# Indirect DMAs in place of the gather and scatter products of seven expert units

## The chip, the cores and the metric

The kernel runs on one core of a Trainium2 chip. The metric is the device time of one execution in microseconds (us).

## The reference, cut to what matters

Two transformer layers on 256 tokens of width 1024 with 16 meta tokens ahead of them. The second layer ends in a top-2-of-8 mixture of experts, and then a final RMSNorm:

```python
logits = (x @ w_router).astype(jnp.float32)
top_v, top_i = lax.top_k(logits, TOP_K)
gates = jax.nn.softmax(top_v, axis=-1)
combine = jnp.sum(jax.nn.one_hot(top_i, N_EXPERTS) * gates[..., None], axis=1)
for e in range(N_EXPERTS):
    out = out + combine[:, e:e + 1] * _swiglu(x, w_gate[e], w_up[e], w_down[e])
```

All numbers are float32; an expert has 1024 x 3584 gate and up weights and 3584 x 1024 down weights.

## The kernel before

All weights stream from HBM once, in chunks of 128 x 4096 numbers (2 MB), through three buffers `raw`. ScalarE rounds a chunk to fp32r (`wh`, L627 for the experts), VectorE subtracts and rounds the rest (`wl`, L993), and TensorE (PE) makes three products with the rounded parts of the activations: high by high, high by low, low by high. `wh` and `wl` have two buffers each. SP issues the next load into a `raw` buffer as soon as VectorE has finished with it (L374 for the experts).

Layer 0 and the attention of layer 1 go first. GpSimd does nothing there but issue a few loads of constants. Then the router's logits are made, each token's two best experts are found, and each token gets its place among the tokens of each expert (`pos`, 1 to 128 within a unit, 0 for none). This ends with the semaphore `routed`.

The experts are worked through in units. A unit is one expert with up to 128 of its tokens; an expert with more tokens gets a further unit, so there are 8 to 11 of them, and their number is read from memory as `units`. The loop over units runs on PE, ScalarE, VectorE and SP at once, one body each, tied by semaphores that count per unit. A unit has 21 chunks, in the order g0, u0, then g, u and d of the one before for six rounds, then d6 in two halves (22 pieces). In one unit, on PE:

- `up(i, "g")` and `up(i, "u")` (L1610, L1611, L1616): gate and up products of one chunk, 24 matmuls of 512 columns. ScalarE makes SiLU of the one, VectorE multiplies with the other (L1131).
- `turn(i)` (L1653): four transposes of that activation, rounded into `eah` (ScalarE, L662) and `eal` (VectorE).
- `down(i)` (L1630, L1631, L1638): 24 matmuls into PSUM banks 2 and 3.
- `gather(u + 1, half)` (L1586): the next unit's tokens, as columns. The tokens `tok` lie in SBUF as rows; a 0/1 matrix `pick` that VectorE builds from `pos` (L1046) is the other operand. Each half is 16 matmuls; half 0 stands after the fourth turn of activations, half 1 after the last. ScalarE and VectorE round the result into `gh` and `gl`.
- the scatter (L1685): the unit's output `y`, copied from banks 2 and 3 by ScalarE (`output_out`, L657), is multiplied by `payT`, which holds each token's gate at its slot. Four fp32 products go to PSUM and VectorE adds them into `acc` (`add_unit`, L1113), while the next unit runs. `payT` comes from `pay` (VectorE, L1146) by two transposes (L1669) and a copy (L686).

PE works in order. At a unit's end it runs gather half 1, both halves of d6, waits for ScalarE's copy of `y`, runs the four scatter products and begins the next unit. ScalarE's order at that place is: rounding of piece 0 of the next unit, `output_out`, rounding of piece 1. VectorE's is: subtraction of piece 0, one of the four additions, subtraction of piece 1, and the other three additions later.

Of the kernel before, what the change touches and what calls it, by code (L numbers as in the profile page):

```python
# [26 lines left out]
F32 = mybir.dt.float32  # L27
# [17 lines left out]
E = 8  # L45
# [39 lines left out]
MAX_UNITS = E + 3  # L85


SUMS = (4, 7, 5, 6)
# [28 lines left out]
def constants():  # L117

    r = np.arange(P)
    ident = np.eye(P, dtype=np.float32)  # L120
    from_here = (r[:, None] >= r[None, :]).astype(np.float32)
    ones = np.ones((P, P), np.float32)
    before = (r[:, None] < r[None, :]).astype(np.float32)
    strict = np.where(r[:, None] < r[None, :], np.float32(0), np.float32(MASKED)).astype(np.float32)
    causal_bias = np.zeros((P, L), np.float32)
    causal_bias[:, L - P:] = np.where(r[None, :] <= r[:, None], 0.0, MASKED)
    swap = np.zeros((P, P), np.float32)
    swap[r, r ^ 32] = 1.0
# [6 lines left out]
    return {  # L135
        "c_base": np.concatenate([ident, ones], 1),
        "c_stick": np.concatenate([-from_here, -ones, ident, strict[:, 0:KT2[2]], strict], 1).astype(np.float32),
        "c_diff": np.concatenate([causal_bias, swap, cos, sin], 1).astype(np.float32),
        "c_route": np.concatenate([before, slots, desc, E - desc], 1).astype(np.float32),
    }  # L140


def build(nc, x, meta, gains, sb_qkv, sb_o, d_qkv, d_o, subln, lq1, lk1, lq2, lk2,
          ffn_gate, ffn_up, ffn_down, router, moe_gate, moe_up, moe_down, final_norm,
          c_base, c_stick, c_diff, c_route, out):
    ctx = ExitStack()
    with ctx:
# [27 lines left out]
        wr = sb("wr", [P, KD, E])  # L175
        xn3 = xn[:].rearrange("p (k t) -> p k t", t=L)
        nd = DIFF_HEADS * SEQ

# [38 lines left out]
        def experts(own):  # L217
            b = {}
            for name, shape in (("tok", [P, QT, D]), ("acc", [P, QT, D]), ("pick", [P, QT, P]), ("pay", [P, QT, P]),
                                ("payT", [P, SEQ]), ("sil", [P, BANK]), ("act", [P, BANK]), ("y", [P, D]),  # L220
                                ("r", [P, 10, QT, E]),
                                ("one", [P, 8, QT]), ("pos", [P, QT, 12]), ("gate", [P, QT, 12]),
                                ("over", [P, 20, E]), ("unit_f", [P, 16])):
# [3 lines left out]
            b["unit_i"] = sb("unit_i", [1, 16], I32, where=own)  # L227
            return b

# [53 lines left out]
        y_ev, sc_done, acc_done = sem("y_ev"), sem("sc_done"), sem("acc_done")  # L283
        fin_sq, fin_root, fin_ready = sem("fin_sq"), sem("fin_root"), sem("fin_ready")

        def cols(w, i):
# [106 lines left out]
        @block.gpsimd  # L393
        def _(pool):
            pool.dma_start(soft_row[:, 0:3 * P + DIAG], c_stick).then_inc(stick_in, 16)
            pool.dma_start(rcon[:], c_route).then_inc(route_in, 16)
            pool.dma_start(wr[:], router[0].rearrange("(k p) e -> p k e", p=P)).then_inc(route_in, 16)

            pool.wait_ge(w_used, C_D_QKV)
            pool.dma_start(b1["con"][:], c_diff).then_inc(diff_in, 16)  # L400

            pool.wait_ge(logit_done, 1)
            pool.wait_ge(back_done, 8)
            pool.dma_start(xn[:, 0:D], final_norm[None, :].to_broadcast([P, D])).then_inc(gain_in, 16)


        @block.scalar
        def _(act):
# [250 lines left out]
            with act.Fori(0, units) as u:  # L659
                def turned_high(i):  # L660
# [3 lines left out]

                with act.If(u > 0):
                    unit_split(u, 0)
                    output_out(u)
                    unit_split(u, 1)
                for j, (kind, i) in enumerate(unit_chunks):
# [10 lines left out]
                    if kind == "d" and i + 1 < FC:  # L680
                        turned_high(i + 1)
                        if i + 1 == FC - 1:
                            unit_split(u, PIECES - 1)
                        if i + 1 == 3:
                            act.wait_ge(payT_done, u + 1)
                            act.copy(bm["payT"][:], ps[:, 7, 0:SEQ]).then_inc(payT_ev, 1)  # L686
                        if i + 1 == FC - 1:

                            gathered_high(u + 2)

            output_out(units)
# [12 lines left out]
        def _(dve):  # L704
# [396 lines left out]
            step(ins)  # L1101
            dve.wait_ge(routed, 1)
# [3 lines left out]
            dve.nop().then_inc(acc_done, 4)  # L1106
# [8 lines left out]
            with dve.Fori(0, units) as u:  # L1115
# [4 lines left out]
                with dve.If(u > 0):  # L1120
                    unit_split(u, 0)
                    add_unit(u, 0, 1)
                    unit_split(u, 1)
                for j, (kind, i) in enumerate(unit_chunks):
# [9 lines left out]
                    if j + 2 < CPU:  # L1134
                        unit_split(u, j + 2)
                    if (kind, i) == ("u", 0):
                        with dve.If(u > 0):
                            add_unit(u, 1, 4)
                    if kind == "d" and i + 1 < FC:
                        turned_low(i + 1)  # L1140
                        if i + 1 == FC - 1:
                            unit_split(u, PIECES - 1)
                        if i == 1:

# [3 lines left out]
                            ins.then_inc(pay_ready, 1)  # L1148
                        if i == 2:
                            dve.wait_ge(gathered, u * 2 + 2)  # L1150
                            pick(u + 1)
                        if i + 1 == FC - 1:
                            gathered_low(u + 2)
            add_unit(units, 0, 4)

# [10 lines left out]
        def _(pe):  # L1166
# [426 lines left out]

            pe.nop().then_inc(sc_done, 4)
            pe.wait_ge(routed, 1)
            units = pe.value_load(bm["unit_i"][0:1, 15:16], min_val=E, max_val=MAX_UNITS)
            with pe.Fori(0, units) as u:
                gh, gl = bm["gh"], bm["gl"]
# [20 lines left out]
                def down(i, k0=0, n=4):  # L1619
# [23 lines left out]
                def turn(i):  # L1643

                    pe.wait_ge(eprod_ready, u * FC + i + 1)
                    if i:
                        pe.wait_ge(eal_ready, u * FC + i)
                    else:

# [6 lines left out]
                for i in range(FC):  # L1656
# [5 lines left out]
                    if i >= 1:  # L1662
                        down(i - 1)
                        turn(i)
                    if i == 3:
                        pe.wait_ge(pay_ready, u + 1)
# [4 lines left out]
                    if i == 4:  # L1671

                        gather(u + 1, 0)

                gather(u + 1, 1)
                down(FC - 1, 0, 2)
                down(FC - 1, 2, 2)
                pe.wait_ge(payT_ev, u + 1)

                pe.wait_ge(gl_ready, u * 2 + 4)  # L1680
                for n in range(4):
                    half, t = n // 2, n % 2
                    if t == 0:
                        pe.wait_ge(y_ev, u * 2 + half + 1)
                    pe.matmul(ps[:, SUMS[n], :], bm["payT"][:, t * P:(t + 1) * P],  # L1685
                              bm["y"][:, half * BANK:(half + 1) * BANK], start=True, stop=True).then_inc(sc_done, 1)


# [19 lines left out]
```

## Time and profile before

| | |
|---|---|
| time, median of 3 runs | 1607.09 us (1605.15 to 1608.3) |
| the profiled execution | 1607.7 us, its span 1605.5 us |
| granted TensorE clock, mean of the span | 0.981 |
| PE, VectorE, ScalarE, GpSimd busy | 1542.0, 1170.3, 938.6, 3.4 us |
| weights' queue | 422.79 MB |
| unit starts, the first matmul of the first and of the last | 562.5 and 1466.1 us |

The span runs from the first to the last instruction of the execution that was profiled; the time of that execution is 2.2 us longer. "Busy" is the union of an engine's instructions. PE stands for matmuls, PEld for its weight loads, DVE for VectorE, ACT for ScalarE, POOL for GpSimd, SPq for the queue of SyncE from which the weights are loaded. An arrow in brackets names what ended an engine's idle time.

### The profile page before, as it was taken

The page shows a single profiled execution, that of the slowest core. Times are in us where ns is not written, and L with a number is a line of the kernel's source. Part 1 is how long each engine was busy: PE and PEld are TensorE (multiplying, and loading weights), DVE is VectorE, ACT ScalarE, POOL GpSimd, SP SyncE. Part 2 cuts the span into 40 slices and gives each one's busy share as a digit, 9 for nine tenths or more (in the row PEclk, how much of TensorE's full clock was granted, in tenths as well). Part 3 has the DMA queues.
Part 4 walks back from the last instruction along what each step waited for, and adds up shares of the span by engine and source line. Part 5 has one row for each costly group of instructions (what it writes and reads, how often), then busy time and mean ns, then how long its engine had stood idle before and what let it go on. Part 6 is the DMA issues. An engine that isn't in the chain of part 4 may idle for free.

```text
span 1605.5 us, 21014 instructions
## 1 busy us (share of the span) xinstructions
PE 1542.0 (96%) x8451; PEld 1311.4 (82%) x8451; DVE 1170.3 (73%) x927; ACT 938.6 (58%) x674; POOL 3.4 (0%) x9
## 2 busy tenths in 40 slices
PE   4999999998987999999999999999999999999997
PEld 4999999998975978878878878878887887887885
DVE  4545756536765578788878878878878878787886
ACT  4454543524236566576666666666666656666664
POOL 0000000000000000000000000000000000000000
PEclk9999999999987899999999999999999999999999
DMA  7444353552530289999989999989999998998993
GB/s 200 119 145 158 128 187 108 210 197 103 209 106 1 81 310 341 347 329 358 343 324 352 344 335 355 366 292 357 337 332 350 370 344 298 361 348 324 359 337 122
DMA packets 198057, 424.93 MB, mean 265 GB/s; under 512 B 3737, under 2 KB 30522, under 8 KB 198010
## 3 DMA queue, kind: packets, MB, share of 16 engines
q1 hardware_dynamic: 197568, 422.79, 73.1%
q0 software_dynamic: 384, 1.45, 0.3%
q8 instruction: 35, 0.57, 0.2%
q14 instruction: 12, 0.10, 0.0%
q10 hardware_dynamic: 58, 0.02, 0.0%
HBM read 423.19 MB, written 1.05 MB: 264 GB/s over the span
## 4 chain that ended last, share of the span: by engine, by line
PE 85%; DVE 7%; ACT 4%; DMA 3%; issue 1%; SPq 0%; DVEq 0%; ACTq 0%
PE ps L1610 12%; PE ps L1611 12%; PE ps L1616 12%; PE ps L1638 6%; PE ps L1190 6%; PE ps L1631 6%; PE ps L1630 6%; PE ps L1181 5%; PE ps L1180 5%; DMA raw<-in_moe_w_down 3%; DVE wl L993 2%; PE ps L1685 2%; PE ps L1586 2%; PE ps L1249 1%; PE ps L1653 1%; DVE wl L720 1%
## 5 line engine op out<-in xcount | busy, mean ns | idle before, releaser
L993 DVE TENSOR_TENSOR wl<-raw,wh 128x4096 fp32r<-128x4096 f32 (+1 forms) x176 | 744.5, 4230 | 167.4 <-ACT wh L627 156.7
L627 ACT CAST wh<-raw 128x4096 fp32r<-128x4096 f32 (+1 forms) x176 | 611.9, 3477 | 308.9 <-PE ps L1611 120.1
L1610 PE MATMUL ps<-wh,gh 128*128 128x512 f32 x896 | 362.1, 404 | 2.0 <-DVE gl L1078 2.0
L1611 PE MATMUL ps<-wh,gl 128*128 128x512 f32 x896 | 355.0, 396 | 0.0
L1616 PE MATMUL ps<-wl,gh 128*128 128x512 f32 x896 | 227.3, 396 | 0.0
L1610 PEld LDWEIGHTS ps<-wh,gh 128*128 128x128 f32 x896 | 169.0, 189 | 42.2 <-issue 3.9
L1611 PEld LDWEIGHTS ps<-wh,gl 128*128 128x128 f32 x896 | 169.1, 189 | 39.9 <-issue 1.7
L1616 PEld LDWEIGHTS ps<-wl,gh 128*128 128x128 f32 x896 | 168.2, 188 | 40.9 <-DVE wl L993 0.2
L1630 PE MATMUL ps<-wh,eah 128*128 128x512 f32 x448 | 177.9, 397 | 0.0
L1631 PE MATMUL ps<-wh,eal 128*128 128x512 f32 x448 | 177.0, 395 | 0.0
L417 ACT CAST wh<-raw 128x4096 fp32r<-128x4096 f32 (+2 forms) x36 | 118.2, 3284 | 82.8 <-PE ps L1181 66.5
L720 DVE TENSOR_TENSOR wl<-raw,wh 128x4096 fp32r<-128x4096 f32 (+2 forms) x28 | 115.2, 4118 | 67.3 <-ACT wh L417 44.8
L1180 PE MATMUL ps<-xh,wh 128*128 128x272 f32 (+1 forms) x544 | 140.4, 292 | 0.2 <-DVE xl L727 0.2
L1181 PE MATMUL ps<-xl,wh 128*128 128x272 f32 (+1 forms) x544 | 137.4, 289 | 0.0
L1638 PE MATMUL ps<-wl,eah 128*128 128x512 f32 x448 | 115.3, 396 | 0.4 <-DVE wl L993 0.2
L1180 PEld LDWEIGHTS ps<-xh,wh 128*128 128x128 f32 x544 | 102.3, 188 | 1.1 <-DVE xl L727 0.6
L1181 PEld LDWEIGHTS ps<-xl,wh 128*128 128x128 f32 x544 | 102.2, 188 | 0.4
L1638 PEld LDWEIGHTS ps<-wl,eah 128*128 128x128 f32 x448 | 83.8, 188 | 22.1 <-DVE wl L993 2.2
L1630 PEld LDWEIGHTS ps<-wh,eah 128*128 128x128 f32 x448 | 84.2, 188 | 20.1
L1631 PEld LDWEIGHTS ps<-wh,eal 128*128 128x128 f32 x448 | 84.2, 188 | 19.8
L1190 PE MATMUL ps<-xh,wl 128*128 128x272 f32 (+1 forms) x544 | 74.6, 296 | 3.3 <-DVE wl L720 3.3
L1190 PEld LDWEIGHTS ps<-xh,wl 128*128 128x128 f32 x544 | 72.1, 196 | 4.1 <-DVE wl L720 3.7
(259 smaller groups left out, 1614.6 us busy)
## 6 DMA issues: line engine op xcount, KB each, us to landing
raw<-in_moe_w_gate SPq DMA_DIRECT2D x56, 2048.0 KB, 8.4
raw<-in_moe_w_up SPq DMA_DIRECT2D x56, 2048.0 KB, 8.8
raw<-in_moe_w_down SPq DMA_DIRECT2D x56, 2048.0 KB, 8.1
raw<-in_sb_w_qkv SPq DMA_DIRECT2D x24, 512.0 KB, 6.1
raw<-in_diff_w_qkv SPq DMA_DIRECT2D x6, 2048.0 KB, 8.1
raw<-in_ffn_w_gate SPq DMA_DIRECT2D x5, 2048.0 KB, 7.9
raw<-in_ffn_w_up SPq DMA_DIRECT2D x5, 2048.0 KB, 7.8
raw<-in_ffn_w_down SPq DMA_DIRECT2D x5, 2048.0 KB, 7.7
```

The costliest lines, as they stand in the source:

```text
L627: act.copy(wh[:, p % 2, 0:to], raw[:, slot, s:s + to]).then_inc(wh_ready, 1)
L720: dve.tensor_tensor(wl[:, c % 2, 0:n], raw[:, c % 3, 0:n], raw_f(wh[:, c % 2, 0:n]), ALU.subtract).then_inc(wl_ready, 1)
L993: dve.tensor_tensor(wl[:, p % 2, 0:to], raw[:, slot, s:s + to], raw_f(wh[:, p % 2, 0:to]), ALU.subtract).then_inc(wl_ready, 1)
L1180: pe.matmul(outp(m), w, highs(k), start=first and k == 0, stop=False, skip_group_check=True)
L1181: ins = pe.matmul(outp(m), w, lows(k), start=False, stop=False, skip_group_check=True)
L1190: ins = pe.matmul(outp(m), w, highs(k), start=False, stop=last and k == k_tiles - 1, skip_group_check=True)
L1610: pe.matmul(ps[:, bank, :], gh[:, s], w, start=(k == 0), stop=False)
L1611: ins = pe.matmul(ps[:, bank, :], gl[:, s], w, start=False, stop=False)
L1616: ins = pe.matmul(ps[:, bank, :], gh[:, s], low[:, k * WIDE:(k + 1) * WIDE], start=False, stop=(k == KD - 1))
L1630: pe.matmul(ps[:, 2 + h, :], ah[:, s], w, start=(i == 0 and k == 0), stop=False)
L1631: ins = pe.matmul(ps[:, 2 + h, :], al[:, s], w, start=False, stop=False)
L1638: ins = pe.matmul(ps[:, 2 + h, :], ah[:, s], w, start=False, stop=(i == FC - 1 and k0 + k == 3))
```

## The change

Two tensors in HBM are added: `token_slots` (11 x 128 rows of 1024) and `output_slots` (8 x 128 rows), and a constant of zeros, `c_zero` (128 x 1024). The constant `STORED` is 7.

- Before layer 0 is over (once PE has used four weight chunks), GpSimd copies the zeros from HBM to HBM, to the slots of units 1 to 7 and to the last 128 rows of `output_slots`: eight copies of 512 KB.
- After `routed`, GpSimd computes for each token and each of its two choices the row of its slot, in small operations, each of which waits for the one before. Four indirect DMAs write all tokens to `token_slots`.
- For each of the units 1 to 7 GpSimd loads the unit's 128 rows into SBUF (`slot_rows`). PE transposes them (`turn_slots`, eight transposes) where the gather was.
- The output `y` of the units 0 to 6 is stored to `output_slots`; no `pay`, `payT`, `pick`, scatter products or additions are made for them.
- In unit 7 GpSimd fetches each token's output rows by four indirect DMAs, multiplies them by the gates and adds them to `acc`. VectorE waits for this (`pooled`) before its own additions.
- Unit 7 and any units after it keep the scatter as before, and the gather for the unit behind them. The loop is split in two on PE, ScalarE and VectorE: `Fori(0, STORED)` and `Fori(STORED, units)`.

```diff
+            pool.wait_ge(w_used, 4)
+            for u in range(1, STORED + 1):
+                pool.dma_start(token_slots[u * P:(u + 1) * P, :], c_zero).then_inc(zero_rows, 16)
+            pool.dma_start(output_slots[STORED * P:(STORED + 1) * P, :], c_zero).then_inc(zero_rows, 16)
...
+            pool.wait_ge(routed, 1)
+            pool.tensor_scalar(here, numbers, float(P), -1.0, ALU.mult, ALU.add)
+            step(pool.tensor_scalar(there, over[:, 1], float(P), float(P * (E - 2) - 1), ALU.mult, ALU.add))
+            step(pool.tensor_tensor(there, there, here, ALU.subtract))
+            for t in range(QT):
+                step(pool.tensor_scalar(place[:, 2 + t], bm["pos"][:, t, 0:E], P + 0.5, None, ALU.is_gt))
+                step(pool.tensor_tensor(place[:, 2 + t], place[:, 2 + t], there, ALU.mult))
+                step(pool.tensor_tensor(place[:, 2 + t], place[:, 2 + t], bm["pos"][:, t, 0:E], ALU.add))
+                step(pool.tensor_tensor(place[:, 2 + t], place[:, 2 + t], here, ALU.add))
+                for choice in range(2):
+                    step(pool.tensor_tensor(place[:, 4 + 2 * t + choice], place[:, 2 + t], r[:, 2 if choice == 0 else 5, t],
+                                            ALU.mult))
...
+            pool.wait_ge(zero_rows, 16 * (STORED + 1))
+            pool.wait_ge(back_ev, 4)
+            for t in range(QT):
+                for choice in range(2):
+                    pool.indirect_dma_start(token_slots, token_row(2 * t + choice), bm["tok"][:, t, :], None).then_inc(spread_in, 16)
+            pool.wait_ge(spread_in, 64)
+            pool.nop().then_inc(y_free, 1)
+            for u in range(1, STORED + 1):
+
+                if u >= 2:
+                    pool.wait_ge(slots_used, u - 1)
+                pool.dma_start(slot_rows, token_slots[u * P:(u + 1) * P, :]).then_inc(slots_in, 16)
+
+                pool.wait_ge(y_ev, 2 * u + 2)
+                pool.dma_start(output_slots[(u - 1) * P:u * P, :], bm["y"][:]).then_inc(y_stored, 16)
+                pool.wait_ge(y_stored, 16 * u)
+                pool.nop().then_inc(y_free, 1 if u < STORED else 1 + MAX_UNITS)
+
+
+            pool.wait_ge(gates_ready, 1)
+            pool.wait_ge(acc_ev, 4)
+            for t in range(QT):
+                for choice in range(2):
+                    pool.indirect_dma_start(flat[:, choice * D:(choice + 1) * D], None, output_slots,
+                                            token_row(4 + 2 * t + choice)).then_inc(fetched, 16)
+                pool.wait_ge(fetched, 32 * (t + 1))
+                for choice in range(2):
+                    part_ = flat[:, choice * D:(choice + 1) * D]
+                    step(pool.tensor_scalar(part_, part_, bm["one"][:, 6 + choice, t:t + 1], None, ALU.mult))
+                    step(pool.tensor_tensor(bm["acc"][:, t, :], bm["acc"][:, t, :], part_, ALU.add))
+            pool.nop().then_inc(pooled, 1)
...
             def output_out(u):
 
                 act.wait_ge(w_used, u * PIECES + C_MOE)
+                act.wait_ge(y_free, u)
...
             def add_unit(u, first, end):
 
+                dve.wait_ge(pooled, 1)
...
+            with dve.Fori(0, STORED) as u:
+                with dve.If(u > 0):
+                    unit_split(u, 0)
+                    unit_split(u, 1)
+                unit_body(u, False)
+            with dve.Fori(STORED, units) as u:
+                unit_split(u, 0)
+                with dve.If(u > STORED):
+                    add_unit(u, 0, 1)
+                unit_split(u, 1)
+                unit_body(u, True)
...
+            def turn_slots(u, half):
+
+                pe.wait_ge(slots_in, u * 16)
+                for f in range(4 * half, 4 * half + 4):
+                    ins = pe.transpose(ps[:, 5 + half, f % 4 * P:(f % 4 + 1) * P], slot_rows[:, f * P:(f + 1) * P], ident)
+                ins.then_inc(gathered, 1)
+                if half:
+                    pe.nop().then_inc(slots_used, 1)
...
+                    if i == 0:
+
+                        pe.wait_ge(y_ev, u * 2 + 2)
...
-                        gather(u + 1, 0)
-
-                gather(u + 1, 1)
+                        if scatter:
+                            gather(u + 1, 0)
+                        else:
+                            turn_slots(u + 1, 0)
+
+                if scatter:
+                    gather(u + 1, 1)
+                else:
+                    turn_slots(u + 1, 1)
                 down(FC - 1, 0, 2)
                 down(FC - 1, 2, 2)
+                if not scatter:
+                    return
                 pe.wait_ge(payT_ev, u + 1)
```

## Rows read from the trace of the kernel before

**Rows 1.** Page: busy time of each engine, share of the span, instructions.
```profile
PE 1542.0 (96%) x8451; PEld 1311.4 (82%) x8451; DVE 1170.3 (73%) x927; ACT 938.6 (58%) x674; POOL 3.4 (0%) x9
```

**Rows 2.** Page, groups: line, engine, operation, count, busy us, mean ns, idle before.
```profile
L1610 PE MATMUL ps<-wh,gh 128*128 128x512 f32 x896 | 362.1, 404 | 2.0 <-DVE gl L1078 2.0
```

**Rows 3.** Windows of two units: PE, PEld, DVE, ACT, POOL busy (count), PEclk, DMA share, GB/s.
```profile
821.60:950.50 128.90, 128.22 (x577) 102.46 (x575) 105.68 (x47) 85.46 (x42) 0.00 (x0) 1.00 0.93 342
...
1208.60:1337.30 128.70, 128.03 (x576) 102.57 (x575) 105.65 (x47) 85.46 (x42) 0.00 (x0) 1.00 0.94 342
```

**Rows 4.** Chain that ended last, in time order: start us, us, what.
```profile
865.91 1.86 PE ps L1638 x8
...
938.87 0.44 PE ps L1653 x4
```

**Rows 5.** Waits of ScalarE's rounding: who for whom, us in total, times, longest.
```profile
ACT wh L627 <- PE ps L1611: 120.1, 60, 5.4
ACT wh L627 <- DMA raw<-in_moe_w_up: 55.9, 24, 4.4
ACT wh L627 <- DMA raw<-in_moe_w_down: 54.2, 28, 4.0
ACT wh L627 <- DMA raw<-in_moe_w_gate: 37.9, 22, 3.6
```

**Rows 6.** Timeline of PE at the end of the third unit: start us, us, instruction.
```profile
945.59 1.10 PE L1638 MATMUL ps<-wl,eah 128*128 128x512 f32 x4
...
950.50 0.79 PE L1610 MATMUL ps<-wh,gh 128*128 128x512 f32 x1
```

**Rows 7.** Timeline of ScalarE, the same place.
```profile
941.63 1.08 ACT L643 CAST gh<-ps 128x512 fp32r<-128x512 f32 x2
942.99 3.63 ACT L627 CAST wh<-raw 128x4096 fp32r<-128x4096 f32 x1 [0.28 <-PE ps L1631]
```

**Rows 8.** Timeline of VectorE, in the middle of that unit.
```profile
858.42 4.43 DVE L993 TENSOR_TENSOR wl<-raw,wh 128x4096 fp32r<-128x4096 f32 x1 [1.00 <-ACT wh L627]
```

**Rows 9.** DMA issues of 850 to 940 us: count, KB each, median us to landing.
```profile
raw<-in_moe_w_gate SPq DMA_DIRECT2D x5, 2048.0 KB, 9.6
raw<-in_moe_w_up SPq DMA_DIRECT2D x5, 2048.0 KB, 10.4
```

**Rows 10.** Timeline of ScalarE, first and last of 13 roundings in that stretch.
```profile
861.16 3.64 ACT L627 CAST wh<-raw 128x4096 fp32r<-128x4096 f32 x1 [2.27 <-DMA raw<-in_moe_w_gate]
...
934.11 1.91 ACT L627 CAST wh<-raw 128x2048 fp32r<-128x2048 f32 x1 [1.38 <-DMA raw<-in_moe_w_down]
```

**Rows 11.** Timeline of ScalarE, in the unit from 1208.6 us.
```profile
1276.42 3.63 ACT L627 CAST wh<-raw 128x4096 fp32r<-128x4096 f32 x1 [1.87 <-PE ps L1611]
```

**Rows 12.** A window of 5 us, the columns of rows 3.
```profile
853.00:858.00 5.00, 5.00 (x23) 4.04 (x22) 4.42 (x2) 3.25 (x1) 0.00 (x0) 1.00 1.01 383
```

**Rows 13.** DMA issues of the whole run: count, KB each, median us to landing.
```profile
raw<-in_moe_w_gate SPq DMA_DIRECT2D x56, 2048.0 KB, 8.4
...
raw<-in_sb_w_qkv SPq DMA_DIRECT2D x24, 512.0 KB, 6.1
...
out<-tok SPq DMA_DIRECT2D x2, 512.0 KB, 2.7
...
xn<-in_final_norm POOLq DMA_DIRECT2D x1, 512.0 KB, 3.8
```

**Rows 14.** Timeline in layer 0: three loads by SP, ScalarE's rounding of them.
```profile
66.68 2.20 SPq L357 DMA_DIRECT2D raw<-in_sb_w_qkv  x3
...
82.81 2.76 ACT L417 CAST wh<-raw 128x3072 fp32r<-128x3072 f32 x1
```

**Rows 15.** Chain in the first unit: the first half gather.
```profile
645.05 1.79 PE ps L1586 x16
```

**Rows 16.** Timeline of VectorE before the units: a small dependent step.
```profile
547.70 0.17 DVE L1010 TENSOR_SCALAR small<-small 128x2 f32<-128x2 f32 x1
```

**Rows 17.** One line of VectorE: ns min/median/max, first and last start us.
```profile
L1161 DVE SCALAR_TENSOR_TENSOR tok<-acc,small,xn x2: 1279/1282/1285, 1599.8 to 1601.0; 128x1024 f32<-128x1024 f32 x2
```

More of the change, by code:

```diff
@@ L85 @@
 MAX_UNITS = E + 3
+STORED = E - 1
 SUMS = (4, 7, 5, 6)
@@ L139, in constants @@
         "c_route": np.concatenate([before, slots, desc, E - desc], 1).astype(np.float32),
+        "c_zero": np.zeros((P, D), np.float32),
     }
@@ L227, in experts @@
             b["unit_i"] = sb("unit_i", [1, 16], I32, where=own)
+            b["row_i"] = sb("row_i", [P, 8], I32, where=own)
             return b
@@ L404, in _, with step @@
             pool.dma_start(xn[:, 0:D], final_norm[None, :].to_broadcast([P, D])).then_inc(gain_in, 16)
+            steps = [0]
+            def step(ins):
+                steps[0] += 1
+                ins.then_inc(pool_step, 1)
+                pool.wait_ge(pool_step, steps[0])
+            r, over, place = bm["r"], bm["over"], bm["place"]
+            row_f, row_i = bm["row_f"], bm["row_i"]
+            numbers = rcon[:, 2 * P + E:2 * P + 2 * E]
+            here, there = place[:, 0], place[:, 1]
@@ new lines, in _, with token_row @@
+            for half in (4, 2):
+                step(pool.tensor_tensor(place[:, 4:8, 0:half], place[:, 4:8, 0:half], place[:, 4:8, half:2 * half], ALU.add))
+            step(pool.tensor_tensor(row_f[:, 0:4], place[:, 4:8, 0], place[:, 4:8, 1], ALU.add))
+            step(pool.tensor_scalar(row_f[:, 4:8], row_f[:, 0:4], float(STORED * P), None, ALU.min))
+            step(pool.tensor_copy(row_i[:], row_f[:]))
+            def token_row(c):
+                return bass.IndirectOffsetOnAxis(ap=row_i[:, c:c + 1], axis=0)
@@ L655, in output_out, with unit_body @@
                 act.wait_ge(w_used, u * PIECES + C_MOE)
+                act.wait_ge(y_free, u)
                 for h in range(2):
                     act.copy(bm["y"][:, h * BANK:(h + 1) * BANK], ps[:, 2 + h, :]).then_inc(y_ev, 1)
-            with act.Fori(0, units) as u:
+            act.nop().then_inc(y_ev, 2)
+            act.nop().then_inc(payT_ev, STORED)
+            def unit_body(u, scatter):
                 def turned_high(i):
@@ L683, in _ @@
                             unit_split(u, PIECES - 1)
-                        if i + 1 == 3:
+                        if scatter and i + 1 == 3:
                             act.wait_ge(payT_done, u + 1)
@@ L1113, in add_unit, with unit_body @@
                     dve.tensor_tensor(a, a, ps[:, SUMS[n], :], ALU.add).then_inc(acc_done, 1)
-            with dve.Fori(0, units) as u:
+            def unit_body(u, scatter):
                 def turned_low(i):
@@ L1135, in _ @@
                         unit_split(u, j + 2)
-                    if (kind, i) == ("u", 0):
-                        with dve.If(u > 0):
+                    if scatter and (kind, i) == ("u", 0):
+                        with dve.If(u > STORED):
                             add_unit(u, 1, 4)
@@ L1142, in _ @@
                             unit_split(u, PIECES - 1)
-                        if i == 1:
+                        if scatter and i == 1:
                             for t in range(QT):
@@ L1148, in _ @@
                             ins.then_inc(pay_ready, 1)
-                        if i == 2:
+                        if scatter and i == 2:
                             dve.wait_ge(gathered, u * 2 + 2)
@@ L1647, in turn @@
                         pe.wait_ge(eal_ready, u * FC + i)
-                    else:
+                    elif scatter:
                         pe.wait_ge(acc_done, u * 4 + 1)
@@ L1664, in _ @@
                         turn(i)
-                    if i == 3:
+                    if scatter and i == 3:
                         pe.wait_ge(pay_ready, u + 1)
@@ L1683, in _ @@
                     if t == 0:
-                        pe.wait_ge(y_ev, u * 2 + half + 1)
+                        pe.wait_ge(y_ev, u * 2 + half + 3)
                     pe.matmul(ps[:, SUMS[n], :], bm["payT"][:, t * P:(t + 1) * P],
                               bm["y"][:, half * BANK:(half + 1) * BANK], start=True, stop=True).then_inc(sc_done, 1)
+            with pe.Fori(0, STORED) as u:
+                unit_body(u, False)
+            with pe.Fori(STORED, units) as u:
+                unit_body(u, True)
 _INS = ["x", "meta_tokens", "norm_gains", "sb_w_qkv", "sb_w_o", "diff_w_qkv", "diff_w_o", "diff_subln",
```

42 lines of the change are left out of this document (29 added, 13 removed).

## Prediction

> **What bounds the kernel now.** I read the page first: TensorE (PE) is busy 96% of the span, VectorE 73%, ScalarE 58% [rows 1]. Then the groups by line: the gate and up products occur 896 times, and one expert unit issues 2 x 7 x 8 = 112 of each, so eight units run, and the three overflow units are empty. So the change's new path serves units 0 to 6, and unit 7 keeps the old gather and scatter [rows 2]. Two whole units last 128.9 and 128.7 us at a granted clock of 1.00 (2.4 GHz), with PE busy 128.2 and 128.0 us of it [rows 3]: PE is the bound of a unit. A unit is 21 weight pieces of 2 MB; each asks for 24 products, eight take 1.86 us, so 5.60 us a piece and, with a third of the 0.44 us that four transposes take, 5.75 us [rows 4].
>
> Second, who is next? The same windows show the 16 DMA engines 93% busy at 342 GB/s [rows 3], and ScalarE's waits before it rounds a piece end on a DMA 74 times in 176 (24+28+22) and on PE's products by the second rounded part 60 times [rows 5]. PE is not late for it yet: it is idle 0.7 us of a unit. So a supply line (load, round on ScalarE, subtract on VectorE, three buffers) runs just ahead of PE. The change shortens PE's work alone, so this line decides what is kept.
>
> **What is removed, per unit, on PE.** (a) Half a gather is 16 products in 1.79 us, both halves 3.58 us; eight transposes at 0.11 us (0.44 for four) take 0.88 us: -2.7 us [rows 4, 15]. (b) The scatter: the last down product ends at 945.59 + 1.10 = 946.69, then PE waits for ScalarE's copy of the output, runs the scatter, and the next unit begins at 950.50: -3.8 us [rows 6]. (c) Two transposes of the payload, half of that 0.44: -0.2 us. Together 6.7 us, so PE alone would need 128.8 - 6.7 = 122.1 us.
>
> **What takes its place at the unit's boundary.** ScalarE rounds the next unit's first piece from 942.99 to 946.62, after its gather evictions end at 942.70 [rows 7]. It cannot start much earlier even though PE gets there 1.35 us earlier (the second half gather): 942.7 to 946.3. PE then is ready at 945.3 and waits 1.0 us; VectorE's subtraction takes 4.43 us behind that [rows 8], to 950.8, while PE's 16 high products (3.73 us) end at 950.1: 0.7 us more. So a new bubble of 1.75 us, and a clean unit takes **123.8 us, -5.0**.
>
> **What the supply line allows.** The loop over three buffers is a load's latency L, 3.63 us of rounding, 4.43 us of subtraction and some 0.3 us of hand-over, thus (L + 8.4)/3 per piece. L is 8.4 us in the median [rows 13], 5.6 us a piece. But in 850 to 940 us it was 9.6 and 10.4 us [rows 9]: at 10, 6.1 us a piece. There ScalarE started 13 pieces in a row behind DMAs, from 861.16 to 934.11, 12 steps of 6.08 us [rows 10]. PE wanted 5.75: 4.0 us lost, which PE never felt, because it had started 3 us behind the line (a subtraction that ends at 862.85 is used at 865.91) [rows 4, 8] and the gather gave 1.8 us back. Six of eight units have such a stretch; in two (the one from 1208.6 us is one) ScalarE keeps waiting for PE [rows 11]. Afterwards gather and scatter give back less. A disturbed unit then lies between 123.8 (all still covered) and 21 x 6.08 = 127.7 us (none); I take the middle, 125.8. Mean: (2 x 123.8 + 6 x 125.8)/8 = 125.3 us, **3.5 us less, times 7 = 24.5 us**.
>
> The Trainium skill, page "DMA: Bandwidth & Descriptors", section "Specifications", gives about 358 GB/s as what HBM allows one core. By that limit a unit with its 45.1 MB would take 126.0 us, an estimate from that page, and the change would keep 2.8 us a unit. The trace speaks against it as a ceiling: a stretch of 5 us moved 383 GB/s [rows 12].
>
> **The added DMAs.** Each unit gets a store of 512 KB and a load of 512 KB. Nearest rows: 2.7 us (out) and 3.8 us (GpSimd's load of the final norm) to landing [rows 13]. Both are issued in the first 10 us of a unit, where ScalarE waits 3.5 us and less for PE. Bounds: 0 to 2.7 us per unit; I take 0, the cover being that wait. If it is gone, 7 x 2.7 = 19 us come back. The eight copies of zeros (512 KB each, HBM to HBM) start when PE has done four pairs, at about 67 us, with the load of the next weights. That load's chunk is rounded at 82.8 us, and such a load lands in 6.1 us [rows 13, 14], 8 us early. Eight copies at 2.7 to 3.8 us are 22 to 30 us of traffic; at half share the load would still just make it: 0, bound +8.
>
> **Waits added.** GpSimd: after routing (561 us) it runs 20 small dependent steps, four scatters and a slot load. PE first wants the slots at 645.05, in place of the gather [rows 15]. One of VectorE's tiny steps takes 0.17 us [rows 16]; at 1 us each on GpSimd, 20 steps, 4 x 3.8 and 3.8 end at 600 us: 45 us early, cost 0. ScalarE's wait for a free output buffer and, queued behind it, the rounding of piece 1: the store was issued a unit earlier, 0. PE's new wait before the first down product: the copies are over some 15 us before it, 0. In unit 7 GpSimd fetches four times 512 KB and runs eight operations of 128x1024, while VectorE works; nearest row 1.28 us for one on VectorE [rows 17]. VectorE losing none or all of it: 0 to 10 us; I take 3, since up to 3 us of lead cover the first two. VectorE also loses 3.6 us of small work per unit (payload, pick, four additions); it does not end the chain: 0. The tail is unchanged.
>
> **Sum.** The profiled execution took 1607.7 us (span 1605.5); the median is 1607.09, 0.04% less, which I neglect. 1607.7 - 24.5 + 3 = **1586 us**.
>
> **Rivals.**
> (1) Clean gain: the line settles at L = 7.8 to 8.4 and PE's floor is reached: 1607.7 - 7 x 5.0 = 1572.7. For it: two units do so already. Against: a faster PE asks for loads sooner, so more of them queue. Chance 0.14.
> (2) The supply line becomes slower than before. Place: the three-buffer loop. It decides from L = 3 x 6.13 - 8.4 = 10.0 us (21 x 6.13 = 128.8). At 10.4, as in the window above, 6.27 us a piece, 131.7 us a unit: +2.9 x 7, so 1628 us. For it: 9.6 and 10.4 in the worst stretch, plus 1 MB more per unit. Against: loads at 8.4 in the median, and each boundary still gives a pause. 0.08 beyond break-even; another 0.08 for near it, 1597 to 1610.
> (3) GpSimd's steps wait for VectorE. In the trace GpSimd computes nothing in the units, so this isn't seen. Price: one step per subtraction, 20 x 5.75 = 115 us, ends at 676, then 19 us of DMAs: 695, where PE stood at 645 since 561. It stalls 50 us: 1586 + 50 = 1636. It decides from (84 - 19)/20 = 3.2 us a step. Chance 0.05: of each 5.75 us, 1.3 us are free of the subtraction, enough for a step or more.
> The Trainium skill, "SBUF — State Buffer", "Who interferes with whom", states this rule: a DVE instruction with two SBUF inputs contends with a GpSimd instruction that reads SBUF, and the subtraction is such a one; no row here shows it.
> (4) That it doesn't do what it says: only if the unit count weren't eight; [rows 2] exclude it.
>
> **Numbers.** Forecast 1586 with 0.65, its own range 1578 to 1597. Measurement can tell some 0.2% (3.2 us). Faster: 0.65 + 0.14 + 0.05 of the near-break-even case = 0.84; same 0.03, the rest of that case; slower 0.08 + 0.05 = 0.13. The range 1572 to 1603 leaves out the slow rivals and a tail of the clean case.
>
> **What would show it.** Right: unit periods near 125 us; ScalarE's waits for DMA grow well above the 148 us of now, those for PE shrink; PE shows waits for the rounded and subtracted weights of 1 to 4 us a unit, 1.7 of it at the boundary; load latency median 9 or more. Clean: latency stays 8.4. Wrong: PE waiting for slot loads in unit 0, for GpSimd at the end, or VectorE's subtraction lasting over 4.4 us in unit 7.

## The result and the profile after

The changed kernel takes 1610.72 us (median of 12 runs, 1609.04 to 1617.55), the kernel before 1605.47 us on the same chip (12 runs, 1603.31 to 1608.3): ratio 1.0033, 95% interval [1.0022, 1.0043], so slower by 0.3%. The forecast was 1586 us, in a range of 1578 to 1597. The profiled execution took 1609.04 us, its span is 1607.2 us.

The page: busy time of each engine (as [rows 1]), and of its DMA issues the weights of the experts and the new transfers (count, KB each, median us to landing, as [rows 13]).

```profile
PE 1512.6 (94%) x8213; PEld 1277.8 (80%) x8213; DVE 1154.3 (72%) x871; ACT 936.5 (58%) x667; POOL 87.0 (5%) x67
...
raw<-in_moe_w_gate SPq DMA_DIRECT2D x56, 2048.0 KB, 9.2
raw<-in_moe_w_up SPq DMA_DIRECT2D x56, 2048.0 KB, 9.1
raw<-in_moe_w_down SPq DMA_DIRECT2D x56, 2048.0 KB, 9.3
...
xn<-token_slots POOLq DMA_DIRECT2D x7, 512.0 KB, 7.2
output_slots<-y POOLq DMA_DIRECT2D x7, 512.0 KB, 5.4
...
hT<-output_slots,row_i POOLq DMA_INDIRECT x4, 11.4
```

TensorE lost 29.4 us of work, and the time did not follow. A load now lands after 9.1 to 9.3 us where it was 8.1 to 8.8. The windows, with the columns of [rows 3], first of units 0 to 6 of the kernel before and its unit 7:

```profile
562.50:1466.10 903.60, 898.64 (x4019) 719.23 (x4019) 738.38 (x337) 597.98 (x288) 0.00 (x0) 1.00 0.93 340
...
1466.10:1605.50 139.40, 128.90 (x576) 102.55 (x574) 107.34 (x53) 82.95 (x46) 0.00 (x0) 0.98 0.76 280
```

and of the changed kernel: units 0 to 6 together, two of them alone, and unit 7.

```profile
560.00:1458.10 898.10, 868.39 (x3780) 685.97 (x3780) 715.25 (x284) 592.30 (x278) 25.68 (x32) 1.00 0.95 350
...
814.10:945.70 131.60, 124.61 (x541) 97.58 (x540) 102.57 (x38) 85.25 (x41) 1.06 (x2) 1.00 0.93 343
...
1075.80:1201.10 125.30, 122.83 (x541) 98.13 (x540) 102.58 (x38) 85.28 (x40) 1.06 (x2) 1.00 0.97 360
...
1458.10:1607.20 149.10, 132.44 (x575) 104.62 (x574) 114.52 (x49) 86.72 (x48) 52.74 (x13) 0.96 0.78 291
```

In seven units PE is busy 30.3 us less (898.64 - 868.39), and they last only 5.5 us less (903.6 to 898.1): 25 us of the gain turned into waiting. Each unit moves the same bytes, some 45.1 MB, so its rate says no more than its length does: 343 GB/s in the slowest unit, of 131.6 us, and 360 in the fastest, of 125.3. Unit 7 lasts 149.1 us where it lasted 139.4: 9.7 us lost. So of two executions the one after is 1.7 us longer in its span, with units that start 2.5 us earlier.

Who waits for whom (as [rows 5]) for ScalarE's rounding, L711 now:

```profile
ACT wh L711 <- DMA raw<-in_moe_w_up: 119.3, 44, 6.3
...
ACT wh L711 <- DMA raw<-in_moe_w_down: 90.8, 44, 4.3
...
ACT wh L711 <- DMA raw<-in_moe_w_gate: 62.5, 43, 3.7
ACT wh L711 <- PE ps L1733: 38.1, 18, 5.4
```

272.6 us behind loads, 131 times of 176, where it was 148.0 us and 74 times; behind PE's products by the second rounded part 38.1 us, where it was 120.1. The supply line now sets the pace for most of the time; e5 to e8 test that. The chain followed back, from 858 to 901 us, shows its loop (start us, us, what):

```profile
858.56 4.44 DVE wl L1090
...
863.15 10.42 DMA raw<-in_moe_w_down
...
873.73 3.63 ACT wh L711
...
877.38 4.43 DVE wl L1090
...
881.98 10.63 DMA raw<-in_moe_w_down
...
892.76 3.63 ACT wh L711
```

Subtraction, load into the buffer set free, rounding, subtraction: 18.82 us from one subtraction to that of the third piece after it (877.38 - 858.56), 6.27 us a piece. That is (10.4 + 8.4)/3, the prediction's formula at the latency of its rival (2). PE needs 5.75 us by the prediction's count.

### The profile page after: what moved, and what is told of

The parts are those of the page before. It is cut to its first block, busy times and chain, and to the rows that moved or that the text cites. A ratio compares the mean times of both kernels' runs of the same rounds, so it can differ in the third digit from the quotient of the medians.

```text
span 1607.2 us, 20460 instructions
## 1 busy us (share of the span) xinstructions
PE 1512.6 (94%) x8213; PEld 1277.8 (80%) x8213; DVE 1154.3 (72%) x871; ACT 936.5 (58%) x667; POOL 87.0 (5%) x67
## 4 chain that ended last, share of the span: by engine, by line
PE 52%; DMA 18%; DVE 16%; ACT 10%; issue 2%; SPq 0%; ACTq 0%; DVEq 0%
DVE wl L1090 12%; DMA raw<-in_moe_w_down 9%; ACT wh L711 8%; DMA raw<-in_moe_w_up 7%; PE ps L1300 6%; PE ps L1738 6%; PE ps L1291 5%; PE ps L1290 5%; PE ps L1732 5%; PE ps L1733 5%; PE ps L1763 3%; PE ps L1755 3%; PE ps L1756 3%; PE ps L1359 1%; DVE wl L817 1%
## 5 line engine op out<-in xcount | busy, mean ns | idle before, releaser
L711 ACT CAST wh<-raw 128x4096 fp32r<-128x4096 f32 (+1 forms) x176 | 611.9, 3477 | 318.2 <-DMA raw<-in_moe_w_up 119.3
L1755 PE MATMUL ps<-wh,eah 128*128 128x512 f32 x448 | 180.4, 403 | 15.5 <-DVE eal L1220 10.4
```

The lines of the kernel that those rows point to most:

```text
L711: act.copy(wh[:, p % 2, 0:to], raw[:, slot, s:s + to]).then_inc(wh_ready, 1)
L1755: pe.matmul(ps[:, 2 + h, :], ah[:, s], w, start=(i == 0 and k == 0), stop=False)
```

## The experiments

Twelve more kernels ran. The table gives the median with its runs, the ratio to the kernel before on the same chip with its interval, and, from each kernel's profiled execution, the mean of units 0 to 6 and the length of unit 7 with the tail (from the first matmul of one unit to that of the next; the last to the end of the span).

| kernel | us (runs) | ratio | unit | unit 7 |
|---|---|---|---|---|
| before | 1605.47 (12) | 1 | 129.1 | 139.4 |
| after | 1610.72 (12) | 1.0033 [1.0022, 1.0043] | 128.3 | 149.1 |
| e1 after, no store or slot load per unit | 1599.18 (5) | 0.9947 [0.9925, 0.9969] | 127.3 | 144.8 |
| e2 after, no arithmetic on GpSimd in unit 7 | 1612.05 (4) | 1.005 [1.0033, 1.0068] | 128.2 | 145.6 |
| e3 after, neither, no fetches | 1591.83 (4) | 0.9917 [0.9901, 0.9934] | 127.3 | 139.1 |
| e4 before, with a store and a load per unit | 1609.29 (10) | 1.0021 [1.0008, 1.0033] | 129.9 | 139.3 |
| e5 after, half of each load | 1568.76 (4) | 0.9772 [0.9756, 0.9788] | 123.6 | 139.2 |
| e6 before, half of each load | 1603.61 (10) | 0.9992 [0.9983, 1.0002] | 128.7 | 139.0 |
| e7 after, four buffers | 1577.02 (4) | 0.9823 [0.9807, 0.984] | 124.2 | 142.7 |
| e8 before, four buffers | 1605.62 (10) | 1.0 [0.9991, 1.001] | 128.7 | 139.0 |
| e9 after, no fetches | 1606.37 (10) | 1.0006 [0.9991, 1.002] | 129.1 | 143.2 |
| e10 four buffers, no fetches or arithmetic | 1574.42 (4) | 0.9812 [0.9797, 0.9827] | 124.5 | 139.2 |
| e11 four buffers, turns moved | 1574.81 (5) | 0.9812 [0.9799, 0.9826] | 124.0 | 142.8 |
| e12 four buffers, no fetches | 1574.38 (4) | 0.9809 [0.9793, 0.9825] | 124.3 | 139.8 |

With three buffers one execution's units vary: the same code of units 0 to 6 gave 128.3, 128.2 and 129.1 us in the profiles of after, e2 and e9. The medians decide there, and they are loose too: e1's runs go from 1591.46 to 1601.28 us, e2's from 1607.80 to 1616.07, e9's from 1601.39 to 1613.50. A difference of two such medians is good to some 4 us. With four buffers all runs of a kernel lie within 2.3 us.

### e1, e2, e3: which part of the change gives the gain back

e1 makes one slot load in place of seven and stores no output, so that the outputs of units 0 to 6 don't reach the result. (It also copies zeros to their rows, seven copies of 512 KB that are over before the units begin.)

```diff
-            for u in range(1, STORED + 1):
...
-                pool.dma_start(slot_rows, token_slots[u * P:(u + 1) * P, :]).then_inc(slots_in, 16)
...
-                pool.dma_start(output_slots[(u - 1) * P:u * P, :], bm["y"][:]).then_inc(y_stored, 16)
+            pool.dma_start(slot_rows, token_slots[P:2 * P, :]).then_inc(slots_in, 16)
```

e2 fetches the rows in unit 7 but leaves out their products and sums; e3 leaves out what e1 and e2 do and the fetches too.

> The changed kernel without the 512 KB store and the 512 KB load of the units 1 to 7 (one load stays, and every unit transposes the same rows; the output rows stay zero, so the experts' outputs of units 0 to 6 are left out). All of PE's, ScalarE's and VectorE's work stays, and so does the combine in unit 7. Theory A, the two transfers at each unit's start push the weight loads back (the load of u1 lands 9 to 10 us after the one before it, and PE idles 2.5 to 7 us a unit): units of 124 to 125.5 us in place of 128.3, the whole 1585 to 1593 us, faster than the kernel before. Rival B, the loop of three buffers cannot go faster than some 6.05 us a piece whatever else is moved: units stay at 127 us or more and the whole above 1600 us.

> The changed kernel without GpSimd's eight multiplications and additions in unit 7 (the fetches stay; the outputs of the units 0 to 6 are left out of the sum). Theory C, these hold VectorE's subtraction back (three of them took 5.8 to 6.6 us in place of 4.43) and PE idles 5 us there: the start of unit 7 to the end goes from 149.1 us to 140 to 144, the whole is 5 to 9 us faster than the changed kernel, so 1602 to 1606 us. Rival: the fetches and the store delay the loads, not the arithmetic: less than 2 us are won.

> Both left out, and the four fetches too. If A and C are right and add up: 124.5 us a unit and 137 us from unit 7's start to the end, 1572 to 1585 us in all, near the clean case of 1572.7. By rival B: above 1595 us.

Without the 13 transfers (seven stores, six of the seven loads) the kernel is 11.5 us faster (1610.72 to 1599.18), 1.6 us a unit: the cover did not hide them. In the profiled executions it is 1.0 us for each of seven units (128.3 to 127.3) and 4.3 in unit 7; of those 4.3, 3.4 are the two falls of the clock in unit 7 of after (last section), which e1's profile doesn't have. Without the arithmetic nothing is gained (1612.05, and the interval of its ratio overlaps that of after). From e1 to e3, which drops fetches and arithmetic, it is another 7.4 us. And e3, where PE's work is as short as in after and none of these transfers is left, still takes 127.3 us a unit and not 123.8.

### e4: the same transfers in the kernel before

> The kernel before, with the change's store of y (512 KB) and a load of 512 KB added in each of units 1 to 7, at the same place, and nothing else. If the cover that the prediction named exists where PE starts a unit behind the supply line by 3 us (that is, in the kernel before), the time stays within 4 us of the kernel before (0 to +4). If a transfer of 512 KB costs DMA time wherever it is (2.7 us for the two), it is slower by 12 to 25 us.

```diff
+            for u in range(1, E):
+                pool.wait_ge(y_ev, 2 * u)
+                pool.dma_start(stored, bm["y"][:]).then_inc(y_stored, 16)
...
+                pool.dma_start(xn[:, D:2 * D], stored).then_inc(slots_in, 16)
```

It costs 4.0 us (1609.29 against 1605.33, interval of the ratio [1.0008, 1.0033]), 0.6 us a unit, less than in after. ScalarE's rounding waits for loads grow here from 148.0 to 264.9 us, nearly to after's 272.6, and the time hardly moves: PE, which starts behind the supply line, covers most of it.

### e5, e6: half of each load

Half of each expert chunk is loaded, the rest of the buffer keeps old weights; every other instruction stays.

```diff
-                    sp.dma_start(dst, src).then_inc(raw_landed[slot], 16)
+                    n_k = src.shape[1] // 2
+                    sp.dma_start(dst[:, 0:n_k], src[:, 0:n_k]).then_inc(raw_landed[slot], 16)
```

> The changed kernel with only the first half of each expert weight chunk loaded (1 MB in place of 2 MB; the other half of the buffer keeps old numbers, so half of the experts' weights is left out). All engine work is the same. Theory B, the supply loop (latency + 8.4)/3 sets the pace of a unit in the changed kernel: a load's latency falls to 5 or 6 us, the loop to 4.6 us a piece, and PE's floor shows: 123.8 us a unit (122.1 of work and 1.7 at the boundary), the whole 1572 to 1585 us. Rival D, PE's new waits come from ScalarE's or VectorE's order of work and not from loads: units stay above 126 us.

> The same halving on the kernel before, as control. PE bounds it, so by theory B nothing moves: units of 128.8 us, the whole 0 to 2 us below the kernel before.

With loads that land after 4.8 to 5.1 us, after runs at 1568.76 us, 34.9 less than before with the same loads (e6); the prediction's clean case was 7 x 5.0 = 35. This is PE's floor: 123.7 us a unit (the first 122.8). ScalarE's rounding waits for PE 150 times in e5 and for a load twice, 4.8 us in all:

```profile
ACT wh L712 <- PE ps L1734: 180.6, 104, 3.8
ACT wh L712 <- PE ps L1757: 77.8, 46, 2.0
```

So the work that was removed is worth all that was said of it, and with full loads it is not kept. Unit 7 loses nothing either (139.2 us), with fetches and arithmetic in it.

### e7, e8: a fourth buffer

Half loads change bytes and latency together. A fourth `raw` buffer, in memory that the attention has left, keeps the bytes and lets a load be issued a piece earlier.

```diff
+        raw3 = phase(lambda own: sb("raw3", [P, CHUNK], where=own))
...
-                return (C_MOE + p) % 3, 0, CHUNK
+                return turns[p], 0, CHUNK
...
+        turns = [0, 1, 2, 3] * 3 + [0, 1, 2] * 3
```

> The changed kernel with a fourth weight buffer in the expert units (16 KB in the place of the dead activations of layer 1; a chunk of three of seven rounds uses it), full loads. Theory B: a loop of 3.4 buffers on average at a latency of 10 us gives (10 + 8.4)/3.4 = 5.4 us a piece, under PE's 5.75, so units near 124 to 125 us and the whole 1578 to 1592 us, faster than both kernels. Rival E, the DMA engines' throughput (6.04 us between landings of queued loads) and not the latency sets the pace: units stay at 127 to 128 us, the whole above 1600 us.

> The same fourth buffer on the kernel before. By theory B it is not the loop that bounds it, so it stays within 2 us of the kernel before; its units go from 129.0 us in the mean to 128.8.

1577.02 us, 33.7 less than after; before gains nothing from it (1605.62). Windows of e7: a unit, units 0 to 6, and unit 7.

```profile
810.60:934.90 124.30, 122.36 (x541) 98.24 (x540) 102.59 (x38) 85.19 (x41) 1.07 (x2) 1.00 0.98 363
...
563.40:1433.00 869.60, 856.45 (x3781) 687.70 (x3781) 715.11 (x285) 592.39 (x279) 29.57 (x32) 1.00 0.97 359
...
1432.90:1575.60 142.70, 129.04 (x575) 102.63 (x574) 115.21 (x49) 86.75 (x48) 57.99 (x13) 0.98 0.81 304
```

and its issues (columns as above):

```profile
raw<-in_moe_w_gate SPq DMA_DIRECT2D x56, 2048.0 KB, 11.9
raw<-in_moe_w_up SPq DMA_DIRECT2D x56, 2048.0 KB, 12.5
raw<-in_moe_w_down SPq DMA_DIRECT2D x56, 2048.0 KB, 12.7
```

A load takes 3 us longer than in after, and the kernel is 2% faster: what after lacked was not throughput but a load in flight. The engines move 359 GB/s over seven units where after moved 350. In the first twelve pieces of a unit, where the fourth buffer takes part, (L + 8.4)/4 lets a piece come every 5.3 us at L = 12.7, below PE's 5.75. The last nine pieces use three buffers again; by position in the unit, the loads of the last six land after a median of 7.6 to 7.9 us, and (7.8 + 8.4)/3 is 5.4. So where the line is ahead of PE its loads land after 7.8 us, at places where they take 8.5 to 9.1 in after.

### e9, e10, e12: fetches or arithmetic in unit 7

> The four indirect fetches of the last unit are left out, so that GpSimd's combine works on what its tiles held; stores, slot loads and all arithmetic stay. Unit 7 to the end took 149.1 us with both, 145.6 without the arithmetic, 139.1 without arithmetic, fetches, stores and slot loads. If the arithmetic costs (VectorE's subtractions of 5.8 to 6.6 us beside it in place of 4.4), unit 7 stays at 147 to 149 and the time at 1609 to 1612 us. If the fetches and the waits for them cost, unit 7 falls to 143 to 145 and the time to 1604 to 1607. The seven units before it are untouched: 128.3 us each by either.

> Four raw buffers, without the fetches and without the arithmetic of the combine; stores and slot loads stay. With four buffers unit 7 to the end took 142.7 us. If what is left of unit 7's loss is the combine and its fetches, unit 7 is 139 to 140 us and the time 1573 to 1574 us; if it is the loads of the last unit themselves, it stays at 142 to 143 and the time at 1577.

> Four raw buffers; the four indirect fetches of the last unit are left out, and the arithmetic stays, on what its tiles held. With four buffers unit 7 to the end took 142.7 us with fetches and arithmetic and 139.2 with neither. If the arithmetic costs, through VectorE's longer subtractions beside it, unit 7 stays at 142 to 143 us and the time near 1577. If the fetches cost, through the loads they delay, unit 7 is 139 to 140 us and the time near 1574.

e9 and e12 leave out the fetches; the arithmetic then works on what its tiles held:

```diff
-                    pool.indirect_dma_start(flat[:, choice * D:(choice + 1) * D], None, output_slots,
-                                            token_row(4 + 2 * t + choice)).then_inc(fetched, 16)
-                pool.wait_ge(fetched, 32 * (t + 1))
```

e10 leaves out the arithmetic too. With four buffers, where the units from the second on repeat within 1 us, it is plain: both out gives unit 7 139.2 us, the fetches out alone 139.8, nothing out 142.7. The arithmetic costs 0.6 us, the fetches the other 2.9, and the medians agree within their spread (1574.42, 1574.38 and 1577.02). With three buffers the medians point the same way: without the arithmetic 1612.05, without the fetches 1606.37, with both 1610.72. The profiles are less plain. e9's unit 7 fell only to 143.2 us, and what is left of it against e3's 139.1 was not taken apart further. e2's took 145.6, 3.5 less than after's, but 3.4 us of after's are the two falls of the clock, which e2's doesn't have.

### e11: the best version

Both halves of `turn_slots` stand behind the last transposes of the activations.

```diff
-                        else:
-                            turn_slots(u + 1, 0)
...
+                    turn_slots(u + 1, 0)
                     turn_slots(u + 1, 1)
```

> Four raw buffers, and the slots' transposes of a boundary both placed behind the last part before the first down half, so that TensorE has them to do while VectorE writes the rounded activations that the down half waits for. With four buffers TensorE is idle 1.0 us there per unit. If that wait can be covered so, idle before the half falls to about 0.6 us, a unit from 124.4 to 124.0 and the whole by 3 us to 1574 us. If the pace with four buffers is still the supply's, or the transposes' copies on VectorE delay the activations as much, it stays at 1577 us.

1574.81 us, 30.7 less than before (ratio 0.9812 [0.9799, 0.9826]); units of 124.0 us. PE's wait ahead of the last down product is 0.6 us in place of 1.04, as expected. It is 2.2 us less than e7, of which the profiled executions show 1.2 in the seven units; the two ran on different chips and the intervals of their ratios overlap. It beats both kernels.

## Why the prediction was wrong

The miss is 24.7 us in the time (1610.72 against 1586), and 26.8 us in the difference: -21.5 us were forecast, +5.25 came. The 2.2 us between the two are the one profiled execution of 1607.7 us that the forecast started from, where the median of before is 1605.47.

**TensorE's saving: right.** 6.7 us a unit were to go, 6.3 went: in e5 PE is busy 854.2 us over seven units, before 898.6. The clean unit was to take 123.8 us; e5's take 123.7, and e7's 124.4. Between the two stand 0.7 us that come back with the full loads.

**The bubble at the boundary: near in size (1.75), most of it at another place.** PE idles 1.6 us in a unit of e5. 0.56 of them are the wait for VectorE's first subtraction, where the prediction had 0.7; the wait of 1.0 us for ScalarE's first rounding isn't there, and one of 1.04 us stands before it. That the sum fits is luck. PE's timeline of after, at the end of the third unit (as [rows 6]), shows this one ahead of the last down products: PE waits for VectorE's rounding of the last activations (`eal`), which 16 matmuls of the gather used to cover and four transposes don't. The prediction took that cover away and set no price on it:

```profile
938.27 0.60 PE L1708 MATMUL ps<-base,xn 128*128 128x128 f32 x4
939.91 0.49 PE L1755 MATMUL ps<-wh,eah 128*128 128x512 f32 x1 [1.04 <-DVE eal L1220]
```

**The supply line: the step that failed.** The prediction had a disturbed unit between 123.8 and 127.7 us, took "the middle, 125.8", and left two units in eight clean. The uncovered end was right for all: e3, which has the shortened units and none of the transfers, needs 127.3 us each and gains 13.5 us (1591.83 against 1605.33), not 24.5. In e3 no unit is clean (126.0 to 128.8 us). The median latency of 8.4 us in before, over all 168 loads of the experts, is 9.3 in e3. Why is argued: the two clean units and the 8.4 us came from a line that often waited for PE before it asked for the next load. What the runs show is the latency where the line waits for PE, 7.6 to 7.9 us in e7's last six pieces, and where it doesn't, 9.3.

**The DMAs at 0: the second step that failed.** "I take 0, the cover being that wait"; measured by e1 it is 1.6 us a unit, 11.5 us in all, within the bound of 2.7. e4 shows that the cover was real in before, where such transfers cost 0.6 us a unit; that the change used it up is argued from there. GpSimd's timeline at the start of the fourth unit of after, and ScalarE's behind it:

```profile
947.15 0.54 POOL L472 DMA_DIRECT2D output_slots<-y  x1 [125.16 <-ACT y L742]
953.33 0.53 POOL L469 DMA_DIRECT2D xn<-token_slots  x1 [5.64 <-DMA output_slots<-y]
```

```profile
951.63 3.63 ACT L711 CAST wh<-raw 128x4096 fp32r<-128x4096 f32 x1 [1.25 <-DMA raw<-in_moe_w_gate]
...
961.04 3.62 ACT L711 CAST wh<-raw 128x4096 fp32r<-128x4096 f32 x1 [5.28 <-DMA raw<-in_moe_w_up]
```

Store and slot load are in flight together with the loads of g1 and u1. ScalarE waited for PE at both in the kernel before:

```profile
954.82 3.63 ACT L627 CAST wh<-raw 128x4096 fp32r<-128x4096 f32 x1 [3.52 <-PE ps L1611]
...
960.42 3.64 ACT L627 CAST wh<-raw 128x4096 fp32r<-128x4096 f32 x1 [1.48 <-PE ps L1611]
```

Now it waits 5.28 us for u1's load. The rows of 2.7 and 3.8 us were taken from transfers with little beside them; here the same 512 KB take 5.4 and 7.2.

**Unit 7: the third.** 3 us were taken, of 0 to 10. From e1 to e3 fetches and arithmetic are 7.4 us. Leaving out the arithmetic alone gained nothing (e2; 0.6 us at most in e12 against e10), leaving out the fetches alone 4.4 (e9) and 2.6 (e12): most of the price is the fetches'. The prediction had priced the arithmetic and the cover for it, and for the fetches it had no term. GpSimd's timeline of after, in unit 7:

```profile
1468.53 4.30 POOL L481 DMA_INDIRECT hT<-output_slots,row_i  x1 [0.30 <-issue]
1479.79 2.85 POOL L486 TENSOR_SCALAR hT<-hT,one 128x1024 f32<-128x1024 f32 x1 [6.95 <-DMA hT<-output_slots,row_i]
```

In the profiled execution PE paused twice for over 2 us, and its clock fell after each pause (below). Unit 7's 9.7 us are 6.2 us more idle time before PE's instructions (7.0 against 0.8) and 3.5 us more busy time (132.44 against 128.90); 3.4 of the latter are the clock.

**The sum.** Against the kernel before: -13.5 (e3) + 7.4 (fetches and arithmetic, e3 to e1) + 11.5 (transfers, e1 to after) = +5.4, measured +5.25. These are steps from one kernel to the next, so they add up by construction, and each is good to some 4 us. The prediction had -24.5 + 3 + 0 = -21.5. So 11.0 us of the miss lie with the middle, 11.5 with the transfers and 4.4 with unit 7.

**The signs.** Of the signs that the prediction named for being right, three came although it was wrong: ScalarE's waits for loads grew, those for PE shrank, the latency rose over 9 us. They told that the line binds, not how much is kept; the unit period, 128.3 and not 125 us, did that. A sign named for being wrong came too, subtractions over 4.4 us in unit 7, and it cost little of the time.

**What held.** The copies of zeros and the start-up cost nothing: units start at 560.0 us where they started at 562.5, and at 560.0 to 563.4 in all profiles of either code. GpSimd's chain of small steps ran from 558.50 to 568.28 us and the first slot load was issued at 589.0, 55 us before PE wants it (644.2): rival (3) is out, though one step did wait out a subtraction (last section). Rival (1) appears only where loads have slack (e5, e7). Rival (2) names what happened, near break-even (1597 to 1610 us) and not far beyond: its mechanism, the three-buffer loop at 10.4 us and 6.27 us a piece, stands in the chain above, but not in every stretch. The seven units still end 5.5 us below those of before; it is unit 7 that carries the whole past break-even.

The Trainium skill's figure of about 358 GB/s (page "DMA: Bandwidth & Descriptors", "Specifications") would have put a unit at 126.0 us, an estimate from that page. That is nearer to after's 128.3 than the forecast's 125.3, but not for its reason: e7 carries 363 GB/s for a whole unit of 124.3 us, above that figure, and a slow unit of after 343, below it. The measurement decides: the rate is not what holds these units.

## What to carry to other kernels

Where a supply line (load, rounding, subtraction) runs just ahead of the bounding engine, its waits for that engine are no reserve that a shorter engine keeps. After the change, take the pace of the stretches where the line already waits for loads, and take it for the whole time. Here a buffer more turned a loss of 5 us into a gain of 28, and was worth nothing before the change. Price new transfers by rows from beside the traffic that they will meet. And test a further buffer before trusting a bandwidth: here each load took 3 us longer, the rate rose from 350 to 359 GB/s and the kernel was 2% faster, so the rate had not been the limit.

## What the runs showed of the hardware

**The clock after a pause.** Windows of 1 us of after in unit 7, while PE pauses 3.14 us and resumes at 1485.2 (columns as [rows 3]):

```profile
1484.00:1485.00 1.00, 0.00 (x0) 0.00 (x0) 0.70 (x2) 0.76 (x2) 1.00 (x1) 1.00 1.06 391
1486.00:1487.00 1.00, 1.00 (x3) 0.78 (x3) 1.00 (x1) 0.60 (x1) 1.00 (x1) 0.50 1.05 385
1489.00:1490.00 1.00, 1.00 (x6) 0.80 (x5) 0.96 (x2) 1.00 (x1) 1.00 (x1) 1.00 0.43 162
```

The granted clock is 1.00 through the pause, 0.50 (1.2 GHz) from 1485 to 1488, then, after a window of 0.79, 1.00 again. The same follows the pause of 2.15 us at 1525.8: 0.50 from 1530 to 1532. Together 3.4 us lost, a price that no wait of the views shows. The length of the pause does not decide it: one of 2.43 us in unit 7 of e2 and one of 2.86 us ahead of the units in e7 left the clock at 1.00 (windows below, e2 and then e7), and one of 2.02 us ahead of the units in before was followed by 0.51. Pauses of 1.0 to 1.4 us in units 0 to 6 of after, and one of 1.74 us in e7, left it at 1.00.

```profile
1487.50:1491.00 3.50, 3.50 (x15) 2.88 (x16) 3.50 (x1) 3.15 (x1) 0.00 (x0) 1.00 1.03 401
```

```profile
563.40:566.80 3.40, 3.40 (x15) 2.77 (x16) 3.40 (x1) 0.16 (x1) 3.40 (x1) 1.00 0.93 378
```

Such a fall costs 1.7 us. The units of before, after and e9 start with one; those of e1, e3 and e7, whose code is after's up to that place or differs from it only in DMAs and buffers, start without. So two profiles can differ by 1.7 us for no reason in the change.

**VectorE and GpSimd hold each other up.** A step of 128x8 on GpSimd takes 0.2 us, and 4.36 us when it meets a subtraction; both end within 0.1 us:

```profile
559.61 0.20 POOL L443 TENSOR_TENSOR place<-place 128x8 f32<-128x8 f32 x1
559.89 4.36 POOL L444 TENSOR_TENSOR place<-place,pos 128x8 f32<-128x8 f32 x1
```

```profile
559.77 4.42 DVE L1090 TENSOR_TENSOR wl<-raw,wh 128x4096 fp32r<-128x4096 f32 x1
```

By the rule that the prediction named (the Trainium skill, "SBUF — State Buffer", "Who interferes with whom") a DVE instruction with two SBUF inputs and a GpSimd instruction that reads SBUF contend, and here the trace agrees; the other 19 steps began outside any subtraction and took 0.3 us at most. In the other direction it appears in unit 7: four of VectorE's subtractions take 4.74 to 6.62 us in place of 4.43, all while GpSimd works through its operations on 128x1024:

```profile
1521.76 6.10 DVE L1090 TENSOR_TENSOR wl<-raw,wh 128x4096 fp32r<-128x4096 f32 x1 [2.04 <-ACT wh L711]
```

e12 has five such, up to 6.03 us, and they cost 0.6 us of its unit 7. e3 and e10, which have no arithmetic on GpSimd, have none: their longest subtraction takes 4.43 us.

**An indirect DMA is slow to issue and to land.** The eight of after hold GpSimd for 0.95 to 4.90 us each while it issues them. The four that write `token_slots` land after a median of 9.6 us, the four fetches of unit 7 after 11.4.
